# A two-layer decoder on one core: seven block products in place of eight in 19 steps of the last down projection

## What is computed

```python
        h = rms_norm(x, ffn_norm_w[l])
        ff = (jax.nn.silu(h @ w_gate[l]) * (h @ w_up[l])) @ w_down[l]
        x = (x + ff).astype(x.dtype)
```

## Time and profile before

| | us |
|---|---|
| median of 3 runs | 2111.05 (2110.71 to 2111.59) |
| the profiled execution, its own time | 2112.05 |
| its span, first to last instruction | 2110.0 |
| PE busy (matmuls) | 2101.6 |
| DVE busy | 1269.3 |
| ACT busy | 983.6 |
| POOL busy | 134.3 |
| DMA: bytes read from HBM, rate over the span | 392.62 MB, 187 GB/s (with 2.13 MB written) |

### The profile page before, as it was taken

How to read it: one execution, slowest core, us unless ns; L and a number is a source line. 1 busy time by engine, 2 the same in 40 slices (tenths; PEclk the granted TensorE clock), 3 DMA queues, 4 the chain that set the end, 5 groups by cost and what they waited for, 6 DMA issues and landing times.

```text
span 2110.0 us, 38413 instructions
## 1 busy us (share of the span) xinstructions
PE 2101.6 (100%) x16853; PEld 1998.7 (95%) x16853; DVE 1269.3 (60%) x1455; ACT 983.6 (47%) x1215; POOL 134.3 (6%) x158
## 2 busy tenths in 40 slices
PE   9999999999999999999999999999999999999999
PEld 8987899999999999999999878999999999988887
DVE  6887866555555555555578878665555555544443
ACT  5555754444444444443445556544444444443332
POOL 1034200000000000000000432000000000000000
PEclk9999999999999999999999999999999999999999
DMA  7675466666666666666666644666666666666664
GB/s 224 181 214 151 128 199 194 197 192 194 195 192 197 192 194 195 192 192 198 192 175 190 199 146 148 193 190 195 194 193 197 192 195 194 192 191 201 198 206 131
DMA packets 204518, 397.24 MB, mean 188 GB/s; under 512 B 12400, under 2 KB 12800, under 8 KB 204352
## 3 DMA queue, kind: packets, MB, share of 16 engines
q1 hardware_dynamic: 202752, 390.24, 62.6%
q0 software_dynamic: 1568, 4.56, 0.9%
q10 hardware_dynamic: 32, 0.01, 0.0%
HBM read 392.62 MB, written 2.13 MB: 187 GB/s over the span
## 4 chain that ended last, share of the span: by engine, by line
PE 98%; DMA 1%; ACT 1%; DVE 0%; issue 0%; SPq 0%; ACTq 0%
PE ps L744 72%; PE ps L547 22%; PE ps L581 1%; PE ps L723 1%; DMA raw<-in_w_in_dram 0%; PE ps L701 0%; PE ps L700 0%; PE ps L676 0%; DMA xr<-in_x_dram 0%; PE ps L661 0%; PE ps L623 0%; PE ps L652 0%; ACT w_hi_s L912 0%; PE ps L559 0%; SPq L326 0%
## 5 line engine op out<-in xcount | busy, mean ns | idle before, releaser
L1169 DVE TENSOR_TENSOR w_lo_s<-raw,w_hi_s 128x1024 fp32r<-128x1024 f32 x553 | 681.7, 1233 | 606.4 <-ACT w_hi_s L912 605.3
L912 ACT CAST w_hi_s<-raw 128x1024 fp32r<-128x1024 f32 x553 | 580.5, 1050 | 783.0 <-PE ps L744 767.7
L744 PE MATMUL ps<-h_hi,w_hi_s 128*128 128x256 f32 x3224 | 892.4, 277 | 1.5 <-DVE h_lo L1178 0.9
L744 PE MATMUL ps<-h_hi,w_lo_s 128*128 128x256 f32 x3224 | 890.8, 276 | 0.0
L744 PE MATMUL ps<-h_lo,w_hi_s 128*128 128x256 f32 x3224 | 890.7, 276 | 0.0
L744 PEld LDWEIGHTS ps<-h_hi,w_hi_s 128*128 128x128 f32 x3224 | 605.5, 188 | 2.1 <-DVE h_lo L1178 1.1
L744 PEld LDWEIGHTS ps<-h_lo,w_hi_s 128*128 128x128 f32 x3224 | 605.5, 188 | 0.0
L744 PEld LDWEIGHTS ps<-h_hi,w_lo_s 128*128 128x128 f32 x3224 | 605.4, 188 | 0.0
L744 PE MATMUL ps<-f_hi,w_hi_s 128*128 128x256 f32 x1192 | 330.3, 277 | 0.0
L744 PE MATMUL ps<-f_hi,w_lo_s 128*128 128x256 f32 x1192 | 329.5, 276 | 0.0
L744 PE MATMUL ps<-f_lo,w_hi_s 128*128 128x256 f32 x1192 | 329.5, 276 | 0.0
(11 more groups left out here) (224 smaller groups left out, 1535.0 us busy)
## 6 DMA issues: line engine op xcount, KB each, us to landing
raw<-in_w_gate_dram SPq DMA_DIRECT2D x176, 512.0 KB, 4.4
raw<-in_w_up_dram SPq DMA_DIRECT2D x176, 512.0 KB, 4.4
raw<-in_w_down_dram SPq DMA_DIRECT2D x176, 512.0 KB, 4.2
raw<-in_w_in_dram SPq DMA_DIRECT2D x144, 512.0 KB, 3.7
raw<-in_w_out_dram SPq DMA_DIRECT2D x64, 512.0 KB, 4.2
cum_all<-cum_kept POOLq DMA_DIRECT2D x8, 512.0 KB, 4.8
xr<-in_x_dram SPq DMA_DIRECT2D x4, 512.0 KB, 9.0
out_dram<-xr SPq DMA_DIRECT2D x3, 512.0 KB, 5.9
```

The source lines that it names most:

```text
L744: done = nc.tensor.matmul(ps[:, bank + m // 2, m % 2 * TOK:(m % 2 + 1) * TOK], w[:, slot, k, m * P:(m + 1) * P], h[:, rows + k, :], start= ...
L912: nc.scalar.copy(split_buffers(pair)[0][:, slot, :, :], raw[:, slot, :, :]).then_inc(hi_split, 1)
L1169: v_.tensor_tensor(lo[:, slot, :, :], raw[:, slot, :, :], hi[:, slot, :, :].bitcast(F32), ALU.subtract).then_inc(lo_split, 1)
```

## The change

In layer 2's down projection two column blocks n = 2 half and 2 half + 1 are worked at once. A step q is two pairs, e = 0 and 1: the same two row blocks of w_down for both n. With two token tiles t this makes a 2 by 2 by 2 product of blocks, eight block products of three matmuls. In 19 of 44 steps (odd q, from 3 in half 0 and from 1 in half 1) it is done in seven block products, by sums of blocks (the Winograd form of Strassen's scheme): 21 matmuls in place of 24.

- The left factor's sums (`left_sums`) are formed by GpSimd in the gate and up chunks of layer 2, split by ACT and DVE (`left_hi`, `left_lo`) and stored to DRAM (`keep_left`), 10 sets of 512 KB. For each seven-product step GpSimd loads its set again (`load_left`).
- The right factor's four sums per step, 128x512 each: GpSimd forms the first two in one instruction (`right_pair_sums`) when both pairs have landed, DVE the other two (`right_sums`), ahead of its split of the step's first pair. ACT and DVE split the four sums in place of the second pair's first half.
- Four banks hold single block sums (`four_banks`), four what is shared (`sum_banks`). The shared ones close with step 19 and are added to x by DVE during steps 20 and 21 (`sums_out`), after ACT has copied one of them (`keep_first`); the others after step 21 (`four_out`). The halves swap the banks, so PE waits for `sums_added` before half 1.
- x is turned back in the first up group of layer 2 (after its pairs 2 and 6), two n at a time, and copied out there by ACT.
- Stores: n = 0 and 1 behind the loads of pairs 54 and 58 of the 88, n = 2 at the end, just before the last two.
- In both layers pair P_FF + 15 uses the weight buffers at the other offset.

```diff
+    STEPS = {0: range(3, 20, 2), 1: range(1, 20, 2)}
+    FORMS = FCH - 1
...
+    def seven(pair):
+        step = down_step(pair)
+        return step is not None and step[1] in STEPS[step[0]]
...
+    def four_banks(half):
+        return [[4, 6], [5, 7]] if half == 0 else [[0, 2], [1, 3]]
+    def sum_banks(half):
+        return (0, 1, 2, 3) if half == 0 else (4, 5, 6, 7)
...
-        FURTHER_ON = (7, 15, 19, 27, P_OUT + 7, P_FF + 7, P_FF + 11, P_DOWN + 3)
+        FURTHER_ON = (7, 15, 19, 27, P_OUT + 7, P_FF + 7, P_FF + 11, P_FF + 15, P_DOWN + 3)
...
+        t_raw = nc.alloc_sbuf_tensor_at("t_raw", [P, 2, 2, N], F32, offset=at_h + 8 * TOK * 4)
...
+        s_ring = h_lo[:, 8:16, :].rearrange("p (r i a) (b c) -> p r i (a b) c", r=2, i=2, b=2)
...
+        s_kept = nc.dram_tensor("s_kept", [FORMS, P, 2, 4, P], F32R, kind="Internal").ap()
...
+                        half, q, e = down_step(layer * PAIRS + p)
+                        n = 2 * half + e
...
-                    if layer == DEPTH - 1 and p >= P_DOWN + DOWN and (p - P_DOWN) % DOWN == 8:
-                        store((p - P_DOWN) // DOWN - 1)
+                    if layer == DEPTH - 1 and p in (P_DOWN + 2 * DOWN + 10, P_DOWN + 2 * DOWN + 14):
+                        store((p - P_DOWN - 2 * DOWN - 10) // 4)
+            store(2)
...
+            def left_sums(c):
+                pool.wait_ge(ff_ready, (DEPTH - 1) * FCH + c + 1)
+                if c:
+                    pool.wait_ge(s_stored, 32 * c)
...
+                a11, a21, a12, a22 = (v[:, i * P:(i + 1) * P] for i in range(4))
+                own.done(pool.tensor_tensor(s_raw[:, 0, :], a21, a22, ALU.add))
+                own.done(pool.tensor_tensor(s_raw[:, 1, :], s_raw[:, 0, :], a11, ALU.subtract))
+                pool.tensor_tensor(s_raw[:, 2, :], a11, a21, ALU.subtract)
+                pool.tensor_tensor(s_raw[:, 3, :], a12, s_raw[:, 1, :], ALU.subtract).then_inc(s_formed, 1)
+            def keep_left(c):
+                pool.wait_ge(s_split, c + 1)
+                pool.dma_start(s_kept[c, :, 0, :, :], s_hi).then_inc(s_stored, 16)
+                pool.dma_start(s_kept[c, :, 1, :, :], s_raw.bitcast(F32R)).then_inc(s_stored, 16)
+            def load_left(half, q):
+                i = seven_before(half, q)
+                if i >= 2:
+                    pool.wait_ge(s_used, i - 1)
+                pool.dma_start(s_ring[:, i % 2], s_kept[q // 2]).then_inc(s_landed[i % 2], 16)
+            def right_pair_sums(half, q):
+                i, pair = seven_before(half, q), (DEPTH - 1) * PAIRS + P_DOWN + 2 * (half * DOWN + q)
+                slot = pair % RING
+                pool.wait_ge(t_split, 2 * i)
+                for j in range(2):
+                    pool.wait_ge(raw_landed[slot + j], 16 * (pair // RING + 1))
+                pool.tensor_tensor(t_raw[:, 0], raw[:, slot + 1, :, :], raw[:, slot:slot + 2, 0, :], ALU.subtract) \
+                    .then_inc(t13_formed, 1)
...
+            pool.wait_ge(s_stored, 32 * FORMS)
+            pool.wait_ge(pair_used, (DEPTH - 1) * PAIRS + P_DOWN + RING)
+            for half in STEPS:
+                for q in STEPS[half]:
+                    load_left(half, q)
+                    right_pair_sums(half, q)
...
+            def seven_products(pair, half, q):
+                i, slot = seven_before(half, q), pair % RING
+                first, last = q == STEPS[half][0], q == STEPS[half][-1]
+                (b11, b12), (b21, _) = four_banks(half)
+                b1, b5, b7, b6 = sum_banks(half)
...
+                def product(bank, left_hi, left_lo, right_hi, right_lo, opens=False, closes=False):
+                    nc.tensor.matmul(ps[:, bank, :], left_hi, right_hi, start=opens, stop=False)
+                    nc.tensor.matmul(ps[:, bank, :], left_lo, right_hi, start=False, stop=False)
+                    return nc.tensor.matmul(ps[:, bank, :], left_hi, right_lo, start=False, stop=closes)
...
+                pe.wait_ge(lo_split, pair + (1 + RING))
+                product(b1, *left(0, 0), w_hi[:, slot, 0, :], w_lo[:, slot, 0, :], first, last)
+                product(b11, *left(1, 0), w_hi[:, slot, 1, :], w_lo[:, slot, 1, :]).then_inc(pair_used, 1)
+                pe.wait_ge(lo_split, pair + (2 + RING))
+                pe.wait_ge(s_landed[i % 2], 16 * (i // 2 + 1))
+                product(b12, *mixed(3), w_hi[:, slot + 1, 1, :], w_lo[:, slot + 1, 1, :]).then_inc(pair_used, 1)
+                pe.wait_ge(t_split, 2 * i + 1)
+                product(b5, *mixed(0), *summed(0, 0), first, last)
+                product(b7, *mixed(2), *summed(0, 1), first, last).then_inc(t_used, 1)
+                pe.wait_ge(t_split, 2 * i + 2)
+                product(b6, *mixed(1), *summed(1, 0), first, last).then_inc(s_used, 1)
+                product(b21, *left(1, 1), *summed(1, 1)).then_inc(t_used, 1)
...
+                        if layer == DEPTH - 1 and c == 0 and q in (2, 6):
+                            if q == 2:
+                                pe.wait_ge(rsb_ready, layer * 2 + 2)
+                            else:
+                                pe.wait_ge(back_ready, 2)
+                            for n in range(q // 2 - 1, q // 2 + 1):
+                                turn_back(n)
+                if layer == DEPTH - 1:
+                    pe.wait_ge(back_ready, DCH)
+                    for half in range(2):
+                        for q in range(DOWN):
+                            pair = base + P_DOWN + (half * DOWN + q) * 2
+                            if half == 0 and q % 2 == 0:
+                                pe.wait_ge(ff_lo, layer * FCH + (q // 2 + 1))
+                            if half == 0 and q == STEPS[0][0]:
+                                pe.wait_ge(gate_scaled, layer * FCH + FCH)
+                                pe.wait_ge(ff_ready, layer * FCH + FCH)
+                            if half and q == 0:
+                                pe.wait_ge(sums_added, 1)
+                            if half and q == STEPS[1][0]:
+                                pe.wait_ge(down_added, layer * DCH + 2)
+                            if seven(pair):
+                                seven_products(pair, half, q)
+                            else:
+                                eight_products(pair, half, q, 0)
+                                if pair + 1 == ALL - 1:
+                                    last_products((pair + 1) % RING, pair + 1, 2 * q, [b[1] for b in four_banks(half)])
+                                else:
+                                    eight_products(pair + 1, half, q, 1)
...
+                if not seven(pair) or down_step(pair)[2] == 0:
+                    nc.scalar.copy(split_buffers(pair)[0][:, slot, :, :], raw[:, slot, :, :]).then_inc(hi_split, 1)
+                    return
+                nc.scalar.copy(w_hi[:, slot, 1, :], raw[:, slot, 1, :]).then_inc(hi_split, 1)
+                i = seven_before(*down_step(pair)[:2])
+                for a in range(2):
+                    act.wait_ge((t13_formed, t24_formed)[a], i + 1)
+                    if i:
+                        act.wait_ge(t_used, 2 * i + a - 1)
+                    nc.scalar.copy(t_hi[:, a], t_raw[:, a]).then_inc(t_hi_ready, 1)
+            def keep_first(half):
+                act.wait_ge(t_used, 2 * seven_before(half, DOWN))
+                nc.scalar.copy(stage[:, 0, 0, :], ps[:, sum_banks(half)[0], :]).then_inc(first_kept, 1)
+            def left_hi(c):
+                act.wait_ge(s_formed, c + 1)
+                nc.scalar.copy(s_hi, s_raw).then_inc(s_hi_ready, 1)
...
+                    if layer == DEPTH - 1 and p in (P_FF + 11, P_FF + 15):
+                        for n in range((p - P_FF - 11) // 2, (p - P_FF - 11) // 2 + 2):
+                            back_out(n)
+                    if layer == DEPTH - 1 and p >= P_FF + PER_FF and (p - P_FF) % PER_FF == 2 and p < P_DOWN:
+                        left_hi((p - P_FF) // PER_FF - 1)
+                    if layer == DEPTH - 1 and p >= P_DOWN and (p - P_DOWN) % (2 * DOWN) == 2 * DOWN - 4:
+                        keep_first(down_step(base + p)[0])
...
+                v_.tensor_tensor(lo[:, slot, 1, :], raw[:, slot, 1, :], hi[:, slot, 1, :].bitcast(F32),
                                  ALU.subtract).then_inc(lo_split, 1)
+                i = seven_before(*down_step(pair)[:2])
+                for a in range(2):
+                    dve.wait_ge(t_hi_ready, 2 * i + a + 1)
+                    v_.tensor_tensor(t_lo[:, a], t_raw[:, a], t_hi[:, a].bitcast(F32), ALU.subtract).then_inc(t_split, 1)
+            def right_sums(pair):
+                slot, i = pair % RING, seven_before(*down_step(pair)[:2])
+                if i:
+                    dve.wait_ge(t_split, 2 * i)
+                dve.wait_ge(t13_formed, i + 1)
+                own.done(v_.tensor_tensor(t_raw[:, 1, 0, :], raw[:, slot + 1, 1, :], t_raw[:, 0, 0, :], ALU.subtract))
```

(92 more changed lines are left out.)

81 lines of the change are left out of this document (46 added, 35 removed).

## The result

The changed kernel takes 2137.78 us in the median (2135.98 to 2140.04), the kernel before 2110.88 beside it: a ratio of 1.0128, 95% interval 1.011 to 1.0145. It is slower by 27 us and lies above the forecast range. Its profiled execution spans 2134.3 us, the one of before 2110.0.

The account below looks back on a forecast made before the run. PE was taken to bound the kernel, busy all of the span; -12.92 saved, +0.6 half 0, +4.3 half 1, +4.0 between the halves, +1.1 end gave -2.9 us: 2108.2 us against 2111.05. Forecast 2105 to 2112 (chance 0.35), whole range 2101.5 to 2119.

Parts of the forecast that it names:

- The missed step: Gate and up of layer 2: the 32 transposes moved there take the same PE time, so 0.
- The saving: Down projection: 19 steps lose three matmuls each, 57 x 0.2267 = 12.92 us off PE.
- The rival that they save nothing: Seven-product steps take as long as eight; waits between the halves and at the end stay: 2116.2 us; chance 0.02.
- The ring: Seven-product steps: loads, GpSimd's sum, DVE's sums and subtraction take 10.78 us per two steps against PE's 10.20.
- the slower rival: Down projection: the left sums' load delays A and B, a step's two raw weight loads; 2117.1 us at e 1.08; chance 0.22.
- e: Excess of the seven-step loop over PE's 10.20 us per two steps: 0.58 us forecast, kept from 0 to 1.1.
- left sums in the way: The same as the slower rival: the left sums' load delays the raw loads, +6.1 us, 2117.1 us; chance 0.22.
- Half 0 and half 1: Down projection: the loop's excess, less slack, costs 0.6 us in half 0 and, with 1.5 for stores, 4.3 in half 1.
- Between the halves: PE waits for DVE to read all four banks of sums before pair 44: 4.0 us.
- the clock rival: TensorE's clock falls in the wait between the halves, costing 2 us: 2110.2 us; chance 0.05.
- The end: Last additions and stores behind the down projection: 0.5 us and 0.6 us, together 1.1 us.
- The rival that they meet in every other step: GpSimd's sum, stretched to 3.5 us by DVE, adds 1.1 us to the ring every other time: 2117 us; chance 0.07.

Follow-up runs that it names:

- experiment 1: The changed kernel with pair P_FF+19 in place of P_FF+15 at the other weight-buffer offset: 2118.9 us, ratio 1.0038.
- experiment 2: The kernel before with only the transposes of x and their copies moved into layer 2's first up group: 2129.0 us, ratio 1.0084.
- experiment 3: The changed kernel with the second transposes two pairs sooner, behind P_FF+12, so P_FF+15 is the third pair behind them: 2121.6 us, ratio 1.005.
- experiment 6: The kernel of experiment 1 with the left sums loaded twice instead of 19 times, so stale sums are multiplied: 2110.9 us, ratio 0.9998.
- experiment 7: The kernel of experiment 1 with GpSimd forming one 128x512 sum more: 2134.6 us, ratio 1.0112.
- experiment 4: The changed kernel with DVE instead of GpSimd forming the first two weight sums: 2120.9 us, ratio 1.0046.
- experiment 5: The changed kernel with DVE reading the four banks of shared sums ahead of its last splits of a half: 2137.8 us, ratio 1.0119.
- experiment 8: The changed kernel with P_FF+19 at the other offset, DVE forming all weight sums and the four banks read first: 2101.06 us, ratio 0.9953.
- experiment 9: The kernel of experiment 8 with the closer second transposes of experiment 3: 2100.79 us, ratio 0.995.
- experiment 10: The kernel of experiment 8 with the transposes of x back in the down projection, 16 behind each of its first two steps: 2100.33 us, ratio 0.9948.

## Why the prediction was wrong

**The missed step.** "The same PE time, so 0" for the transposes moved to gate and up. Their own time is the same, 3.5 us. But they break a stream of stationary weights that, with this list of offsets, doesn't find its pace again, and the 165 pairs of 24 matmuls behind them pay 0.11 us each: 17.5 us, more than the whole change was to bring. Experiments 1 to 3 show it and undo it. The trace of before had the sign: in it the matmuls just behind the norm's four short products are slower,

```profile
1397.90:1403.30 5.40, 5.40 (x47) 5.40 (x47) 2.74 (x4) 1.78 (x2) 1.09 (x3) 1.00 0.64 192
1420.00:1450.00 30.00, 30.00 (x268) 30.00 (x267) 15.77 (x14) 12.61 (x12) 0.00 (x0) 1.00 0.68 193
```

(47 in 5.40 us against 268 in 30.00; the ends count in so short a window, and from start to start it is 0.1178 and 0.1133), and a list called FURTHER_ON in the code, to which the change adds P_FF+15, asks what it is for. I read it as a buffer's place and gave it no price. What I had named as a reason to be wrong, PE waiting in gate and up, isn't there: it doesn't wait, it goes slower.

**The saving.** 57 x 0.2267 = 12.92 us is exact, and the seven products run at the spacing of the others. The rival that they save nothing is out.

**The ring.** Its links, and that PE waits for DVE's split of A, are as told. Without the left sums' loads it measured 10.4 to 10.8 us in half 0 against the 10.78 summed up (experiment 6). The term that failed is the 5.5 us from A's issue to both landings: with the loads it is near 6.0 in half 0, the value of the slower rival, e 1.08 and not 0.58. I had put the left sums' load down to less than half of 1.1 us, since it goes out 2.7 us ahead of A's; it is 2.7 us ahead (issued at 1961.52, A's at 1964.24), and it costs nothing that can be seen or 0.6 to 1.5 us, by when it lands (experiment 7). That the two raw loads before it hold it up was not in the sum. The rival's sum is +6.1; the down projection measured +7.6, without the transposes. So the rival "left sums in the way", to which I gave 0.22, is what happened in the steps, 2117.1 by its sum; experiment 1, which has no slow pace beyond P_FF+19, took 2118.9. That the totals lie so near is in part luck: half 1 and the end came out 3.3 us below the rival's terms, and the clock's 2.4 us and some 2 us of small waits, which it doesn't have, made that good.

**Half 0 and half 1.** 4.3 us of waits at the first products of half 0 and 6.5 in half 1, where the rival's e gave 4.6 and 8.8, the forecast's 0.6 and 4.3. The stores cost more than the 1.5 us summed up: beside the first, A and B had landed only 9.4 us after A's issue, beside the second 7.3, and the longest wait of half 1, 2.18 us, is that of the second one's step. In the steps behind the stores the ring is 11.1 us, e 0.9, and half 1 as a whole stayed below the rival's 8.8.

**Between the halves.** 4.0 us forecast, 5.0 measured. It isn't the arrears of the longer ring: experiment 6, without them, waits 5.2 us there. It is GpSimd's sum for pair 46, which meets one of DVE's additions. The timeline of after:

```profile
1998.71 0.75 DVE L1389 SCALAR_TENSOR_TENSOR xr<-stage,rs,xr 128x512 f32<-128x512 f32 x1
...
2000.78 2.38 POOL L616 TENSOR_TENSOR t_raw<-raw 128x1024 f32<-128x1024 f32 x1 [16.15 <-DMA raw<-in_w_down_dram]
...
2001.23 2.48 DVE L1389 SCALAR_TENSOR_TENSOR xr<-stage,rs,xr 128x512 f32<-128x512 f32 x1
```

An addition of this form takes 0.75 us alone and, beside GpSimd's sum, 2.48. These 1.7 us stand in DVE's queue ahead of the last addition, for which PE waits; without them the wait would be 3.3 us, as an estimate. In experiment 6 the same addition takes 2.38 us; in experiment 4, where GpSimd forms no sum, 0.75, and the wait is 3.7 although DVE has a sum more to form. Then the clock rival came true on top: half clock for 6.8 us, +2.4 us, where I had 2. The Trainium skill, TensorE: Matmul & The Clock Gate, section HAM oscillation, holds that a gap in TensorE's work can halve its clock; the runs agree, with waits of 5.0, 5.2, 3.7 and 2.05 us that were followed by a granted clock of 0.50 for 3.4 to 6.8 us. It isn't every wait: the 2.18 us in after was not followed by one, nor was one of 2.6 in half 0 of experiment 5. Why not, no run shows.

**The end.** 1.1 us forecast, 0.1 measured: 3.8 us behind the last matmul against 3.7.

**GpSimd and DVE.** The rule of the Trainium skill that the two contend (GPSIMD Engine Reference, section Key points) I had weighed and left out of the sum. For the ring that was right: of its 19 sums 17 take 2.38 to 2.40 us, the first 3.19 and one 2.53, with DVE at work beside them. Between the halves it was not: there the trace agrees with the rule, with DVE's addition of 2.48 us for 0.75. The rival that they meet in every other step is out; that they meet once, where PE waits for DVE, cost 1.7 us and wasn't in the sum.

**In sum,** after is slower by a moved break (17.5), a ring with a 512 KB load that at times lands late (e 1.08 in half 0), and a stall between the halves with its clock. With DVE forming the sums, the change is good for 10 to 11 us (experiments 8 to 10) if PE is neither broken into nor made to wait.

## What to carry to other kernels

When work moves into a dense stream of matmuls, its own time is not its price: compare the distance from matmul to matmul behind every break of the kernel that you have, before you call the move free. A sum handed to an idle engine is paid for in the handovers of the ring that it joins; ask first whether the busy engine has room for it, and here it had (85 of 100 us). And a small reload on another queue counts by what it does to the landings of the loads that the ring waits for; look at when it lands, not only at when it is issued.

## What was not expected of the hardware

**Two paces at one clock.** Matmuls of 256 columns start 0.1133 or 0.1178 us apart, in both cases at a granted clock of 1.00 with PE and its weight loads busy throughout. The slower pace is seen behind the breaks by four short products at 1397 us and by 16 transposes, not behind the two small transposes at 1409 in before, and it ends behind a pair whose halves lie 160 bytes further on, if that pair isn't the first behind the break: seen in before (P_FF+7), in experiment 1 (P_FF+19) and in experiment 3 (P_FF+15, now the third behind the break). That pair itself has 0.1167. Why it does so isn't settled: no run changed the offset by another amount, and none put an idle gap in place of the transposes.

**Landings.** Two loads of 512 KB issued 0.6 us apart have both landed 5.2 to 5.5 us after the first issue (half 0 of experiment 6). With a third one 2.7 us ahead of them on another queue it is 5.2 to 5.9 where that one has landed within 1.0 us of the first issue, and 5.9 to 6.8 where it lands later (after). Beside a store of 512 KB between the two it was 9.4.

**The clock.** A wait of 2.05 us was enough to see it halved (experiment 1, at 2033.7), after one of 0.99 us that ended ten us before it. Waits of 2.15 us in the same run and of 2.25 in experiment 5 were not followed by it.

**GpSimd and DVE.** When they meet, either can be the one held up: between the halves of after DVE's addition took 2.48 us for 0.75 and GpSimd's sum 2.38 as ever, at the first sum of the down projection GpSimd took 3.19.
